# A weight ring whose remainder overwrites its raw chunk, loops written out, and a gate block inside the spatial gating

## The reference, cut to what matters

```python
def first_block(...):                      # two layers, l = 0 and 1
    shift, scale, gate = jnp.split(sc @ w_ada[l] + b_ada[l], 3, axis=-1)
    h = rms(x, norm_w[l]) * (1.0 + scale[:, None]) + shift[:, None]
    u = h @ w_in                           # q, k, v of three attentions, gates z
    ...                                    # three attentions: o_a, o_b, o_c
    x = x + gate[:, None] * ((y * jax.nn.silu(z)) @ w_out)

def token_mixer(h, ...):                   # of the second block
    z_sg, q, k, v, og, g_lr, m_a, m_b = jnp.split(h @ w_in, idx, axis=-1)
    u, vs = jnp.split(jax.nn.gelu(z_sg, approximate=False), 2, axis=-1)
    y_a = spatial_gating(u, layernorm(vs, sg_ln_g, sg_ln_b), sg_w, sg_b)
    ...                                    # y_b: gated linear attention in chunks (GLA)
    merged = jax.nn.sigmoid(m_a) * (y_a @ w_proj_a) + jax.nn.sigmoid(m_b) * (y_b @ w_proj_b)
    return merged @ w_out
```

## Time and profile before

| | |
|---|---|
| time, median of 3 runs | 4629.92 us (4622.61 to 4630.57) |
| the profiled execution: time, span | 4635.07 us, 4633.1 us |
| mean granted TensorE clock | 0.887 |
| busy: TensorE, VectorE, ScalarE, GpSimd | 90%, 38%, 36%, 1% |
| TensorE waits for w_lo (line 653) | 83.9 us in 45 waits |
| weights moved by SyncE's queue | 549.39 MB |

### The profile page before, as it was taken

How to read it: one execution, slowest core, us unless ns; L and a number is a source line. 1 busy time by engine, 2 the same in 40 slices (tenths; PEclk the granted TensorE clock), 3 DMA queues, 4 the chain that set the end, 5 groups by cost and what they waited for, 6 DMA issues and landing times.

```text
span 4633.1 us, 53421 instructions
## 1 busy us (share of the span) xinstructions
PE 4149.1 (90%) x19088; PEld 3119.1 (67%) x19088; DVE 1739.8 (38%) x2643; ACT 1676.9 (36%) x2583; POOL 68.8 (1%) x120
## 2 busy tenths in 40 slices
PE   5799979898899989989979889999789987999998
PEld 1466656676566657765657667776267767999876
DVE  0322233322223243333224444443144445666544
ACT  1222223334212133333344444444245455555433
POOL 3000000000001000000000000000000000000000
PEclk7899985569899999985699999999789998999999
DMA  8444420001245433320015545564045544655564
GB/s 272 158 145 145 145 83 0 1 20 29 86 146 164 161 116 110 113 65 0 20 47 147 177 145 164 162 186 145 0 157 162 163 129 126 190 186 186 175 198 154
DMA packets 350494, 575.97 MB, mean 124 GB/s; under 512 B 25252, under 2 KB 130868, under 8 KB 348208
## 3 DMA queue, kind: packets, MB, share of 16 engines
q1 hardware_dynamic: 344000, 549.39, 38.2%
q0 software_dynamic: 6384, 25.14, 1.8%
HBM read 570.26 MB, written 4.19 MB: 124 GB/s over the span
## 4 chain that ended last, share of the span: by engine, by line
PE 52%; DVE 5%; ACT 4%; issue 2%; DMA 0%; DVEq 0%; ACTq 0%
PE ps L653 31%; PE ps L1205 11%; PE ps L745 2%; PE ps L962 1%; DVE w_lo L631 1%; PE ps L736 1%; PE ps L932 1%; ACT w_hi L625 1%; PE ps L1116 1%; PE ps L1109 1%; PE ps L912 1%; PE ps L832 1%; ACT f_arena L1249 0%; PE ps L672 0%; PE ps L986 0%
## 5 line engine op out<-in xcount | busy, mean ns | idle before, releaser
L631 DVE TENSOR_TENSOR w_lo<-raw_ring,w_hi 128x1024 fp32r<-128x1024 f32 (+1 forms) x827 | 1010.1, 1224 | 1653.3 <-ACT w_hi L625 1643.5
L625 ACT CAST w_hi<-raw_ring 128x1024 fp32r<-128x1024 f32 (+1 forms) x827 | 864.0, 1048 | 1779.6 <-PE ps L653 1468.1
L653 PE MATMUL ps<-w_hi,r_a 128*128 128x512 f32 x3552 | 1286.6, 403 | 92.9 <-DVE w_lo L631 66.3
L653 PE MATMUL ps<-w_lo,r_a 128*128 128x512 f32 x2624 | 1042.5, 397 | 0.0
L653 PEld LDWEIGHTS ps<-w_hi,r_a 128*128 128x128 f32 x3552 | 679.8, 191 | 379.9 <-issue 180.7
L653 PE MATMUL ps<-w_hi,r_b 128*128 128x512 f32 x2272 | 864.1, 400 | 15.0 <-DVE w_lo L631 12.3
L653 PEld LDWEIGHTS ps<-w_lo,r_a 128*128 128x128 f32 x2624 | 503.2, 192 | 97.3
L653 PEld LDWEIGHTS ps<-w_hi,r_b 128*128 128x128 f32 x2272 | 435.4, 192 | 122.4 <-DVE w_lo L631 14.2
L1205 PE MATMUL ps<-r_a,w_hi 128*128 128x256 f32 x2816 | 495.5, 281 | 3.0 <-DVE w_lo L631 3.0
L1205 PEld LDWEIGHTS ps<-r_a,w_hi 128*128 128x128 f32 x2816 | 431.5, 190 | 3.4 <-issue 3.2
L1205 PE MATMUL ps<-r_a,w_lo 128*128 128x256 f32 x1408 | 395.2, 281 | 0.0
(11 more groups left out here) (291 smaller groups left out, 3061.5 us busy)
## 6 DMA issues: line engine op xcount, KB each, us to landing
raw_ring<-in_w_in_dram SPq DMA_DIRECT2D x386, 512.0 KB, 3.7
raw_ring<-in_w_ada_dram SPq DMA_DIRECT2D x192, 512.0 KB, 3.8
raw_ring<-in_ffn_w_up_dram SPq DMA_DIRECT2D x176, 512.0 KB, 3.5
raw_ring<-in_w_out_dram SPq DMA_DIRECT2D x96, 512.0 KB, 4.4
raw_ring<-in_ffn_w_down_dram SPq DMA_DIRECT2D x88, 512.0 KB, 4.5
raw_ring<-in_w_proj_b_dram SPq DMA_DIRECT2D x32, 512.0 KB, 3.8
raw_ring<-in_w_proj_a_dram SPq DMA_DIRECT2D x16, 512.0 KB, 3.9
raw_ring<-in_w_qb_dram SPq DMA_DIRECT2D x24, 288.0 KB, 2.9
```

The lines of the kernel that those rows point to most:

```text
L625: nc.scalar.copy(WH[:, ph.s_slot(j), 0:n], RAW[:, ph.raw_slot(j), 0:n]).then_inc(hi_ready, 1)
L631: nc.vector.tensor_tensor(WL[:, ph.s_slot(j), 0:n], RAW[:, ph.raw_slot(j), 0:n], WH[:, ph.s_slot(j), 0:n].bitcast(F32), ALU.subtract).then ...
L653: mm = nc.tensor.matmul(PS[:, ti, 0:cols], X(x, k, t), W[w][:, ph.s_slot(j), kk * cols:(kk + 1) * cols], start=(k == 0 and q == 0), stop=( ...
```

## The change

Four things at once.

1. The remainder is written over its raw chunk: w_lo is a second name for the raw ring's memory. The memory of two w_lo slots becomes one more raw slot and one more w_hi slot: five raw, three high. A raw slot of a split chunk is now free when TensorE has used the pair (`pair_used`).
2. Every loop is written out: `run` and `Fori` go, slots and semaphore values are constants. The assertion on the slots goes too.
3. In the spatial gating, the eight gate chunks of ma's first block are put between its steps: on TensorE chunk 0 before the weights' transposes, chunks 1 to 5 before the wait for `y_in`, chunks 6 and 7 before the transposes of the result. ScalarE's and VectorE's parts are placed to match, and the last gelu of uv stands behind the first high part of ma.
4. SyncE's special case for chunks 7 and 8 of ma and mb goes.

```diff
-RAW_SLOTS, SPLIT_SLOTS = 4, 2
+RAW_SLOTS, SPLIT_SLOTS = 5, 3
...
         RAW = place("raw_ring", RAW_SLOTS * SLOT).rearrange("p (s n) -> p s n", s=RAW_SLOTS)
+        WL = place("w_lo", RAW_SLOTS * SLOT, F32R, offset=base).rearrange("p (s n) -> p s n", s=RAW_SLOTS)
         WH = place("w_hi", SPLIT_SLOTS * SLOT, F32R).rearrange("p (s n) -> p s n", s=SPLIT_SLOTS)
-        WL = place("w_lo", SPLIT_SLOTS * SLOT, F32R).rearrange("p (s n) -> p s n", s=SPLIT_SLOTS)
...
+                        g, ap = ph.g0 + i * ph.m + j, src(i)
+                        if g >= RAW_SLOTS:
+                            k, n = kinds[g - RAW_SLOTS]
+                            sp.wait_ge(pair_used if k == "S" else plain_used, n + 1)
...
-            nc.vector.tensor_tensor(WL[:, ph.s_slot(j), 0:n], RAW[:, ph.raw_slot(j), 0:n],
-                                    WH[:, ph.s_slot(j), 0:n].bitcast(F32), ALU.subtract).then_inc(lo_ready, 1)
+            nc.vector.tensor_tensor(WL[:, ph.raw_slot(i, j), 0:n], RAW[:, ph.raw_slot(i, j), 0:n],
+                                    WH[:, ph.s_slot(i, j), 0:n].bitcast(F32), ALU.subtract).then_inc(lo_ready, 1)
...
-                run(pe, 4, a_body)
+                for i in range(4):
+                    a_body(i)
...
+            def ma_gate(lo, hi):
+                for c in range(lo, hi):
+                    pe_block_part(pe, PH["ma"], 0, S8, c, 2, NB, hT, range(2), AC["ma"][0])
+            ma_gate(0, 1)
             pe.wait_ge(sg_in, 64)
...
+            ma_gate(1, 6)
             pe.wait_ge(y_in, 1)
...
+            ma_gate(6, 8)
             pe.wait_ge(tr_free, TRN["sg"][0] + 4)
...
+            act_hi(act, PH["ma"], 0, 0)
+            uv_evac(3)
+            for j in range(1, 4):
+                act_hi(act, PH["ma"], 0, j)
+            root("ln", SS[:, 0:2], RINV[:, 0:2])
+            for j in range(4, 9):
+                act_hi(act, PH["ma"], 0, j)
+            sig_evac("ma", 0)
+            to_hi("ya", 8, lambda k: YT[:, 0, k, :], 256)
+            sig_loop("ma", 12, 1)
...
+            dve_lo(dve, PH["ma"], 0, 0)
             for k in range(2):
...
+            dve_lo(dve, PH["ma"], 0, 1)
             dve.wait_ge(sg_in, 64)
...
             L(ins)
+            dve_lo(dve, PH["ma"], 0, 2)
             for t in range(2):
                 ins = V.bn_aggr(BNA[:, t, :], BNS[:, t, :])
             L(ins)
+            dve_lo(dve, PH["ma"], 0, 3)
...
             L(ins)
+            dve_lo(dve, PH["ma"], 0, 4)
...
             TT(vs, vs, bc(SGG[:, SGW:2 * SGW], 2), ALU.add).then_inc(y_in, 1)
+            for j in (5, 6):
+                dve_lo(dve, PH["ma"], 0, j)
...
                 ins.then_inc(tr_free, 1)
+            for j in (7, 8):
+                dve_lo(dve, PH["ma"], 0, j)
             split("ya", 8, lambda x, k: YT[:, x, k, :], 256)
```

More of the change, by code:

```diff
@@ L86, in __init__ @@
     def __init__(self, eng, sem):
-        self.eng, self.sem, self.n, self.off, self.k = eng, sem, 0, 0, 0
+        self.eng, self.sem, self.n = eng, sem, 0
     def __call__(self, ins):
-        self.k += 1
+        self.n += 1
         ins.then_inc(self.sem, 1)
[L92 to L127, removed]
+        self.eng.wait_ge(self.sem, self.n)
 def build(nc, A, out, xs):
@@ L848, in ada_body @@
                         pe_ada(pe, PH[name], i, j, j, before + i)
-                        if j == 1 and not (isinstance(i, int) and i == 0):
+                        if j == 1 and i:
                             pe_ada_turn(pe, before + i - 1)
-                run(pe, n, ada_body, peel=1)
+                for i in range(n):
+                    ada_body(i)
                 pe_ada_turn(pe, before + n - 1)
@@ L1274, in body @@
                         act_hi(act, ph, i, j)
-                        if q == 0 and evac and not (isinstance(i, int) and i == 0):
+                        if q == 0 and evac and i:
                             evac(i - 1)
-                run(act, ph.iters, body, peel=peel)
+                for i in range(ph.iters):
+                    body(i)
                 if evac and last:
@@ L1345, in win_body @@
                         for t in range(4):
-                            u_evac(i, t, 4, None if isinstance(i, int) and i == 0 else 4 * i + t - 3)
-                    run(act, 8, win_body, peel=1)
+                            u_evac(i, t, 4, None if i == 0 else 4 * i + t - 3)
+                    for i in range(8):
+                        win_body(i)
                 else:
@@ L1436, in c_body @@
                     act_units(act, UN[f"c{l}"] + i * len(UC), UC, PBC, PTC)
-                run(act, H_C, c_body, link=L, per=T + 3)
+                for i in range(H_C):
+                    c_body(i)
                 ph = PH[f"z{l}"]
@@ L1550, in _ @@
             act.wait_ge(gl_a, 1)
-            run(act, GH, gla_body)
+            for i in range(GH):
+                gla_body(i)
             act.wait_ge(gl_of, 2 * GH + 1)
@@ L1735, in body @@
                         own(i)
-                run(dve, ph.iters, body, peel=1, link=L, per=links)
+                for i in range(ph.iters):
+                    body(i)
                 for fn in (evac, later):
@@ L1778, in ada_block @@
                 return body
-            run(dve, 2, ada_block("ada0", 0))
+            for i in range(2):
+                ada_block("ada0", 0)(i)
             dve.wait_ge(gains_in, 16 * 10)
@@ L1813, in _ @@
                 if l == 0:
-                    run(dve, 6, ada_block("ada0b", 2))
+                    for i in range(6):
+                        ada_block("ada0b", 2)(i)
                     flips()
@@ L2229, in up_body @@
                             fn(pi, pb, q)
-            run(dve, 11, up_body, peel=1, link=L, per=8)
+            for i in range(11):
+                up_body(i)
             for c in range(8):
@@ L2233, in _ @@
                     fn(10, 1, q)
-            run(dve, 2, lambda i: [dve_lo(dve, PH["down"], i, j) for j in range(44)])
+            for i in range(2):
+                for j in range(44):
+                    dve_lo(dve, PH["down"], i, j)
             post("p_ffn", YF, PNF, 48, x_done)
```

214 lines of the change are left out of this document (111 added, 103 removed).

## The result

The changed kernel took 4544.02 us (median of 4 executions, 4529.07 to 4552.54) beside 4626.26 us of the kernel before on the same chip: a ratio of 0.9822, 95% interval 0.9801 to 0.9842. A second set, beside other runs of the kernel before, gave 4536.53 us and 0.9804 (0.9783 to 0.9825). The direction was right, the size was not.

What follows compares the result with a forecast made beforehand. TensorE, busy 90% of the span, was taken as the bound, so only time between matmuls could go: 10 + 14 + 18 + 5 + 1 = 48 us off, giving 4582 us, range 4560 to 4608.

Steps and rivals of the forecast that it cites:

- Fetch and written-out code: Straight code in all stages: some 149 instruction blocks, 1 us gained; rival, fetch stalls make it slower, chance 0.05.
- The feed-forward: Feed-forward's first half, 3863 to 4359 us: TensorE already almost fully busy, so it "has nothing to give".
- First stage: ada0 and ada0b, plain chunks from memory: five raw slots keep five transfers under way, 10 us gained, bounds 0 and 20.
- The gate block: Between uv and ma: gate chunks placed between the spatial gating's steps gain 14 us, bounds 8 and 17.
- Ends of blocks: Stalls where one engine evacuates PSUM, from wout1 to xv: the third high slot's slack gains 18 us (sum 18.3).
- Table loads: ScalarE's table loads on the path go: three in GLA 3.8 us, mb's 1.3, together 5 us; attention 0.
- The sum: Whole kernel: 10 + 14 + 18 + 5 + 1 = 48 us off, giving 4582 us.
- first stage faster, half clock rarer: Rival: first stage reaches 5/4 of the rate and half clock after stalls is rarer, 10 to 15 us more, 4570; chance 0.12.
- the range's low end: Whole kernel: 4560 us, with 20 us gained in the first stage and 12 us more elsewhere.
- waits for w_lo under 65 us: Sign of being right: TensorE's waits for the remainder, 83.9 us before, fall under 65 us.

Runs made afterwards that it cites:

- two_high: Changed kernel with one stricter wait, so high parts are held back as with two high slots, five raw slots kept: 4572.23 us, ratio 0.9880 to the kernel before.
- written_out: Kernel before with loops written out and SyncE's special case gone; ring of four raw, two high slots and gating order as before: 4590.03 us, ratio 0.9922.
- gate: Kernel before with loops written out and the gate block between the gating's steps, old ring of four raw and two high slots: 4592.01 us, ratio 0.9930.
- six_raw: Changed kernel with the same memory as six raw and two high slots instead of five and three: 4564.08 us, ratio 0.9868 to the kernel before.
- ring: Kernel before with loops written out and the ring of five raw and three high slots, spatial gating in its old order: 4554.72 us, ratio 0.9847.
- written_again: Second run of the kernel with only loops and SyncE's special case removed from the kernel before: 4594.24 us, ratio 0.9927.
- early_one: Changed kernel with the next block's first split chunk prepared ahead of the evacuation in win0, z0 and wout0: 4481.62 us, ratio 0.9681 to the kernel before.
- gla_loop: Changed kernel with only ScalarE's body of the gated linear attention (GLA) back in a loop: 4540.63 us, that stage 164.2 us.

## Why the prediction was wrong

**Fetch and written-out code.** Right in mechanism: 151 blocks came, and inside the stages no idle time over 0.3 us is put down to issue. By the Trainium skill (Runtime: NRT & Kernel Launch, Instruction fetch mechanics) sequential fetch is hidden; this trace agrees, with 151 blocks and no stall that can be put down to them.

**The feed-forward, the step that failed most.** The forecast read "97% to 99.9% busy" as full and closed the stage: "has nothing to give". It gave 15 to 19 us. Busy time is the sum of matmuls whose ends are modelled, and a slower pace makes each of them longer (281 ns against 276), so the share stays at 99.9% while 4% of the pace is lost. The view that would have shown it was there: the start times in the trace of before go from 113.3 to 117.8 ns apart at iteration 3. two_high settles that the third high slot restores the pace; what in TensorE makes it fall and stay low is not settled.

**1. First stage: 10 forecast, 16 measured** (mean of written_out, gate and their repeats, 131.5; of the changed kernel's two, 115.8), less 1.2 us by which the first matmul starts later; the forecast had the fifth chunk fit before it for nothing. The mechanism was right, the size was taken "nearer to the idle share than to 5/4", and that was the wrong end: 349 over 285 GB/s is 1.22, and six_raw went on to 382. A DMA share of 0.86 left more than 14% to win.

**2. The gate block: 14 forecast, 15 measured** from uv's last matmul to chunk 8 (36.4 against 51.3 us). Of these, 2.7 came with the loops (written_out: 48.6), as ma's first table load no longer stands on the path, and 0.6 with the ring (48.0); the block itself is 11.6. What reaches qkvo is 9 and 11 us in the two profiles; in the first, the four projection chunks ran for part of their time at half clock (12.6 us against 10.9). In the timed runs it was 11 us with three high slots, within the noise (18 by the second set, clear of it), and nothing with two, which is open.

**3. Ends of blocks: 18.3 forecast, some 25 measured.** wout1 3.3 (2.6 forecast), ma and glr 3.6 (1.7; ring against written_out), mb 3.4 to 3.9 (3), xk and xv 7.1 (5.1), qkvo 5.9 to 6.7 (some 4), uv 1.6 (1.7). The reasons held: mb's 1.11 us fell to 0.23, which is the forecast's 0.85 and a little. Not all of it is ends, though: inside the chunks, too, matmuls on 512 columns come 229.1 ns apart in ring and 230.1 in written_again (means of qkvo), an estimated 1 us of qkvo's 1056 matmuls. That win0, z0 and wout0 would not gain from slots alone was right (wout0's 2.8 us came with the loops; win0 has seven such ends, not eight); it took the engine's order as given, though. early_one shows that with three slots the order was worth 44 us in these stages.

**4. Table loads: 5 forecast, GLA alone gave 9 to 13.** The loads left as foreseen. Mis-sized was what they cost: 1.28 us of idle time each, as forecast, and TensorE's slower clock on top, which the forecast left out; by gla_loop's one execution 7.5 us for three. Some 2.3 us of idle time went with the other engines' loops, and the clock's share varies by up to 9 us between executions of written-out bodies. Attention in layer 1 gave 3 and wout0 2.8 with the loops alone, where 0 was put down; which of registers, branches or loads that was, no run told apart.

**The sum.** By the medians: loops 37 and 33 us (forecast with loads, sigmoids and gelu: about 10), ring 35 (about 24), gate block 11 to 18 (14). The loops' excess lies most in GLA (14 and 18 us between the profiles), the ring's most in the feed-forward (19); the terms come from single profiles and don't add up to the medians exactly. The rival "first stage faster, half clock rarer" at 0.12 was the nearest and named the first stage rightly, but it stopped at 4570, and the feed-forward's slow pace is not half clock (0.99 to 1.00); the range's low end left out what the feed-forward could give, because a step had closed it. Of the signs of being right, "waits for w_lo under 65 us" came out at 59.0 partly by the change of names above.

## What to carry to other kernels

A busy share near 1 doesn't show that a stage is at its pace: compare the distance between the starts of equal instructions early and late in it, and between stages. A stall costs more than its own time where it sends TensorE to half clock: here removing 7 stalls of 2.4 us gave 27 to 29, and three loads of 1.28 us cost 7.5 in the one execution that has them. With a deeper buffer in place, look at the order too: ask at each evacuation which of the next block's preparations can stand ahead of it, and stop at the one that would wait for its transfer.

## What was not expected of the hardware

- Matmuls of 128x128 weights on 256 columns kept one of two paces at the same granted clock, 113.3 or 117.8 ns apart. Past the stage's first two chunks the slow one appeared only where the operand was ready under 0.5 us before its use (never at 2.4 us or more), began at a chunk's boundary, and mostly stayed (43.5 and 45.2 us for 384 matmuls).
- With 4, 5 and 6 transfers of 512 KB under way the core read 285, 349 and 382 GB/s, though the DMA engines' share was already 0.86 and 0.98 with four and five.
- GLA of one kernel took 149.1 and 155.9 us in two executions, on the same work, with a mean clock of 0.79 and 0.75. The windows of written_again and of written_out:

```profile
3193.30:3342.40 149.10, 98.91 (x257) 43.84 (x256) 43.65 (x69) 37.71 (x80) 0.00 (x0) 0.79 0.00 1
```

```profile
3198.10:3354.00 155.90, 105.75 (x257) 46.16 (x255) 43.72 (x69) 37.82 (x80) 0.00 (x0) 0.75 0.00 1
```
